# Two heads at a time on the row halves of TensorE: the sparse scores of a two-layer streaming encoder

## The reference

```python
def _dsa_attend(q, k, v, iq, ik, iw, cid_q, cid_k, k_top):
    sc = jnp.einsum('bqhd,bkd->bqhk', iq, ik).astype(jnp.float32)
    score = jnp.einsum('bqhk,bqh->bqk', jax.nn.relu(sc), iw.astype(jnp.float32)) * IDX_SCALE
    ...
    _, sel = lax.top_k(score, kk)
    ...
    s = jnp.einsum('bqhd,bqsd->bqhs', q, k_sel).astype(jnp.float32) * (HD_C ** -0.5)
    s = jnp.where(valid[:, :, None, :], s, -jnp.inf)
    p = jax.nn.softmax(s, axis=-1).astype(v.dtype)
    return jnp.einsum('bqhs,bqsd->bqhd', p, v_sel)
```

## Time and profile before

| | us |
|---|---|
| median of 3 runs (lowest to highest) | 2138.87 (2136.68 to 2142.58) |
| the profiled execution | 2146.08 |
| its span | 2144.4 |
| TensorE busy | 1932.9 |
| VectorE busy | 1392.8 |
| ScalarE busy | 736.3 |
| mean granted TensorE clock | 0.982 |

### The profile page before, as it was taken

How to read it: one execution, slowest core, us unless ns; L and a number is a source line. 1 busy time by engine, 2 the same in 40 slices (tenths; PEclk the granted TensorE clock), 3 DMA queues, 4 the chain that set the end, 5 groups by cost and what they waited for, 6 DMA issues and landing times. The chain is left out here.

```text
span 2144.4 us, 27310 instructions
## 1 busy us (share of the span) xinstructions
PE 1932.9 (90%) x9670; PEld 1083.1 (51%) x9690; DVE 1392.8 (65%) x2961; ACT 736.3 (34%) x1678; POOL 259.0 (12%) x360
## 2 busy tenths in 40 slices
PE   3999999989999788999959999999899988889997
PEld 2634457555545555654444344565554455565443
DVE  3268488998796776533233684989897956665322
ACT  3353134233212544443243512334331134444332
POOL 0000132342100000001100002233221000000011
PEclk9999999999999999999979999999999999999998
DMA  8201214121323003223351022221205130022242
GB/s 281 99 25 67 79 47 136 61 81 50 113 73 77 18 6 94 89 67 132 128 193 55 25 71 74 92 97 60 96 30 153 38 72 13 26 76 87 95 149 103
DMA packets 151272, 178.34 MB, mean 83 GB/s; under 512 B 71408, under 2 KB 106736, under 8 KB 150864
## 3 DMA queue, kind: packets, MB, share of 16 engines
q1 hardware_dynamic: 123072, 139.19, 20.7%
q10 hardware_dynamic: 28064, 37.38, 4.9%
HBM read 119.72 MB, written 66.69 MB: 87 GB/s over the span
## 5 line engine op out<-in xcount | busy, mean ns | idle before, releaser
L914 PE MATMUL ps<-wring,xnT_arena 128*128 128x512 f32 (+2 forms) x2304 | 921.3, 542 | 0.0
L914 PEld LDWEIGHTS ps<-wring,xnT_arena 128*128 128x128 f32 x2304 | 405.0, 192 | 354.5 <-issue 337.7
L1759 DVE TENSOR_SCALAR_CACHE_REDUCE arena<-arena,theta 32x1056 bf16<-32x1056 f32 x496 | 461.3, 979 | 2.3
L1396 ACT COPY arena<-ps 128x512 f32<-128x512 f32 (+3 forms) x144 | 75.3, 523 | 449.4 <-PE ps L914 415.8
L1274 PE MATMUL ps<-wring,xnT_arena 128*128 128x512 f32 x512 | 223.9, 595 | 0.0
L2043 DVE TENSOR_REDUCE mneg<-ps 128x1 f32<-128x192 f32 (+9 forms) x148 | 113.9, 770 | 87.1 <-PE ps L1206 84.7
L1274 PEld LDWEIGHTS ps<-wring,xnT_arena 128*128 128x128 f32 x512 | 96.4, 191 | 115.4 <-issue 115.4
L1050 PEld LDWEIGHTS ps<-arena 128*128 128x128 f32 x488 | 69.6, 193 | 106.8 <-DVE arena L1866 78.2
L2206 POOL TENSOR_TENSOR arena<-arena 128x1024 f32<-128x1024 f32 (+1 forms) x16 | 35.5, 2216 | 727.2 <-DVE arena L1984 539.1
L1050 PE MATMUL ps<-arena 128*128 128x128 f32 x488 | 80.2, 287 | 39.5 <-DVE arena L1866 39.3
L1361 ACT COPY xnT_arena<-ps 128x512 f32<-128x512 f32 (+3 forms) x84 | 39.0, 464 | 188.9 <-PE ps L1218 141.6
(11 more groups left out here) (270 smaller groups left out, 2495.1 us busy)
## 6 DMA issues: line engine op xcount, KB each, us to landing
projected<-arena ACTq DMA_DIRECT2D x130, 256.0 KB, 2.0
arena<-residual SPq DMA_DIRECT2D x34, 512.0 KB, 5.2
wring<-in_w_in SPq DMA_DIRECT2D x16, 1024.0 KB, 7.6
o_bc<-projected SPq DMA_DIRECT2D x36, 384.0 KB, 3.7
wring<-in_w_in SPq DMA_DIRECT2D x6, 2048.0 KB, 8.8
wring<-in_w_out SPq DMA_DIRECT2D x8, 1024.0 KB, 5.5
residual<-arena SPq DMA_DIRECT2D x16, 512.0 KB, 2.6
out<-arena SPq DMA_DIRECT2D x16, 512.0 KB, 4.0
```

The lines of the kernel that those rows point to most:

```text
L914: o = mm(bank(pbank(k), 0, w_), xnT[:, c, t * P:(t + 1) * P], w, start=(c == 0), stop=(c == CH - 1))
L1396: nc.scalar.copy(stage[s][:, 0:wide], bank(pbank(k), 0, wide)).then_inc(p_ev, 1)
L1759: V.tensor_scalar(cmp_out[0][r, (i % 2) * WMAX:(i % 2) * WMAX + uw[u]], score[u][r], th_, 0.0, op, ALU.add, accum_out=into[r, i:i + 1]).th ...
```

## The change

For the paired tiles of dsa, heads 0 and 1 (then 2 and 3) become one unit of the order. The keys stand twice, on rows 0 to 63 and again on rows 64 to 127. Two heads of queries stand on the same halves, so the queries of a tile need two transposes in place of four. For each run of keys two matmuls of 64 rows follow each other, one head on the upper and one on the lower half of the rows, into different banks. Then the masks of the first head follow, on all 128 rows, and those of the second. The score of tile 8, which has no partner, stays one head at a time but now uses rows 0 to 63 alone, since the other half no longer holds zeros. Fox and unit "s" keep their form.

```diff
+        packed = lambda mu: mu[0] == "dsa" and any(len(group) == 2 and mu[1] in group for group in UNIT_GROUPS)
...
+                elif packed((m, group[0])):
+                    AJ += [(m, u, 2 * g + e) for g in range(2) for u in group for e in range(2)]
...
+            if packed(j[:2]) and j[2] % 2 == 0:
+                score_at.append(max([n - 3] + score_at[-1:] + [i + (0 if i >= n - 1 or packed(AJ[i][:2]) else 1) for k in (n, n + 1) for i in used_before[AJ[k]]]))
...
-                for m, u, h in AJ[max(0, n - 1):n]:
-                    if u == "s" or h % 2:
+                now = [j for i, j in enumerate(AJ) if (j[1] == "s" or j[2] % 2) and n == i + 1 + (packed(j[:2]) and i + 2 < len(AJ) and packed(AJ[i + 2][:2]))]
+                for m, u, h in now:
...
+                                    if u == "p":
+                                        tr(ps[0:HD, 512 * b + P * i:512 * b + P * i + P], src, C("ident"))
+                                        o = mm(ps[HD:P, 512 * b + P * i:512 * b + P * i + P], src, C("ident"), start=True, stop=True, skip_group_check=True)
...
+                            if packed(mu):
+                                for g in range(2):
+                                    o = tr(bank(b, P * g, P), QD_[unit_no[mu] % 2][:, P * g:P * g + P], C("ident"))
...
+                        if packed(mu):
+                            for key, w, col in runs:
+                                for e, h_ in enumerate(heads):
+                                    at = col - base + 512 * banks_of((m, u, h_))[0]
+                                    mm(ps[:, at:at + w], qt[HD * e:HD * e + HD, h // 2, :], dsaKT["p"][HD * e:HD * e + HD, key:key + w],
+                                       start=True, stop=False, skip_group_check=True)
+                        for h_ in heads if packed(mu) else ():
...
+                        if m == "dsa" and u != "s":
+                            qt, kt = qt[0:HD], kt[0:HD]
...
-                        copy(dsaKT["p"][0:HD, 0:HALF], ps[0:HD, 512 * b:512 * b + HALF]).then_inc(own_sem, one_more(own))
+                        copy(dsaKT["p"][:, 0:HALF], ps[:, 512 * b:512 * b + HALF]).then_inc(own_sem, one_more(own))
...
-                    nc.gpsimd.memset(dsaKT["p"][HALF:], 0.0).then_inc(pool_own, one_more(own))
```

More of the change, by code:

```diff
@@ L375, in encoder @@
         AU = [(m, u) for m in ("fox", "dsa") for group in UNIT_GROUPS for u in group]
-        AJ = [(m, u, h) for m in ("fox", "dsa") for group in UNIT_GROUPS for h in (range(H) if group != ["s"] else [0]) for u in group]
+        packed = lambda mu: mu[0] == "dsa" and any(len(group) == 2 and mu[1] in group for group in UNIT_GROUPS)
+        AJ = []
+        for m in ("fox", "dsa"):
+            for group in UNIT_GROUPS:
+                if group == ["s"]:
+                    AJ.append((m, "s", 0))
+                elif packed((m, group[0])):
+                    AJ += [(m, u, 2 * g + e) for g in range(2) for u in group for e in range(2)]
+                else:
+                    AJ += [(m, u, h) for h in range(H) for u in group]
         group_of = {(m, u): (m, i) for m in ("fox", "dsa") for i, group in enumerate(UNIT_GROUPS) for u in group}
@@ L505, in plan_attend @@
             for n, job in enumerate(AJ):
-                seq += [("score", AJ[i]) for i in range(n + 1, len(AJ)) if score_at[i] == n == i - 1]
+                seq += [("score", AJ[i]) for i in range(n + 1, len(AJ)) if score_at[i] == n == i - 1 and not packed(AJ[i][:2])]
                 seq.append(("turn", job))
                 seq += [("exp", AJ[i]) for i in (n + 1, n + 2) if i < len(AJ) and i == (max(n, 0) + 2 if score_at[i] <= i - 3 else n + 1)
-                        and ("exp", AJ[i]) not in seq]
+                        and ("exp", AJ[i]) not in seq and ("score", AJ[i]) in seq]
                 done, backs = backs, []
@@ L526, in plan_attend @@
                 seq += [("back", p) for p in done]
-                seq += [("score", AJ[i]) for i in range(n + 1, len(AJ)) if score_at[i] == n < i - 1]
+                seq += [("score", AJ[i]) for i in range(n + 1, len(AJ)) if score_at[i] == n and (n < i - 1 or packed(AJ[i][:2]))]
+                seq += [("exp", AJ[i]) for i in range(n + 1, len(AJ)) if score_at[i] == n == i - 1 and packed(AJ[i][:2])]
             PV.append((AJ[-1][0], AJ[-1][1], AJ[-1][2] // 2))
@@ L1145, in scores @@
                         mu, n = (m, u), job_no[(m, u, h)]
+                        if packed(mu) and h % 2:
+                            return
+                        heads = (h, h + 1) if packed(mu) else (h,)
                         base = 512 * banks_of((m, u, h))[0]
@@ L1160, in scores @@
                                     evacuated(a)
-                        for i in sorted(used_before[m, u, h]):
+                        for i in sorted(set(i for e in heads for i in used_before[m, u, e])):
                             turned(AJ[i])
```

38 lines of the change are left out of this document (30 added, 8 removed).

## The result

The changed kernel takes 2153.47 us (median of 6 runs, 2150.0 to 2158.11) against 2138.28 before: ratio 1.0071, 95% interval 1.0054 to 1.0087. It is slower by 15 us; 2128 was forecast, at most 2140. The profiled execution of the changed kernel took 2154.23 us (span 2152.6, clock 0.974); that of before, 2146.08, lies 8 above its median, so the two profiles differ by only 8.

What follows compares the result with a forecast made beforehand. TensorE was taken as the bound, with VectorE's queue limiting (1, 5) and (2, 6). Per layer +2.0 - 2.2 + 0.5 - 4.3 - 4.3 + 3.0 = -5.3, both -10.6: 2138.9 to 2128 us, range 2112 to 2140.

Steps and rivals of the forecast that it cites:

- rival C: Slower: more, shorter TensorE waits drop the clock to 1.2 GHz more often, 1.7 us per stretch; 2152 to 2155; chance 9%.
- (1, 5): dsa's pair of tiles 1 and 5: VectorE's queue limits it, so +0.5 us per layer where TensorE's work alone gives -3.0.
- beside the path: Preparations: wider key copies, ScalarE's query scaling, query DMA and the dropped memset add no time; at worst a few tenths.
- (2, 6): dsa's pair of tiles 2 and 6: rounds set by VectorE, long wait cut into several; -4.3 us per layer.
- (3, 7): dsa's pair of tiles 3 and 7: bound by TensorE, keeps its gain; -4.7 + 0.4 for changes = -4.3 us per layer.
- The scores: Paired dsa tiles 0 to 7: two heads abreast halve 27.3 us of score time, -13.65 us per layer.
- Changes of division: Switching TensorE's array between row divisions costs 0.09 us each: +1.5 per layer at paired masks, +2.2 in tile 8.
- tile 8: dsa's unpaired tile: 24 changes of array division and a first score waiting for VectorE's copy; +3.0 us per layer.
- Keys: Second key product for nine dsa tiles, made in fox and partly hidden by a wait: +2.0 us per layer, bounds 0 to 3.7.
- cover: In tiles 3 and 7, the small tile's values, over 1 us, hide the wait for the copy of turned probabilities.
- (0, 4): dsa's pair of tiles 0 and 4: TensorE's work gives -2.1 + 0.4 - 0.4; taken as -2.2 us per layer.
- rival B: Emptying PSUM, one bank set per tile, takes back nearly all gain but that of tiles 3 and 7; 2139; chance 20%.

Runs made afterwards that it cites:

- e2: Changed kernel's order of jobs (two heads as one unit) without halves: all scores on 128 rows, one after the other, keys once; 2149.9 us, ratio 1.0033 to 1.0063.
- e10: Kernel before with only the dsa keys written to both halves of the rows, scores still on 128 rows in the old order; 2144.2 us, ratio 1.0001 to 1.0032.
- e1: Changed kernel with tile 8 scored on all 128 rows again, ScalarE zeroing the upper rows of its queries; 2142.8 us, ratio 1.0006 to 1.0034.
- e3: Kernel before with the scores of all dsa prompt tiles on rows 0 to 63, one head at a time, old order; 2196.4 us, ratio 1.0196 to 1.0292.
- e17: Kernel before with the dsa scores of tiles 3 and 7 alone on rows 0 to 63, old order; 2144.0 us, ratio 1.0015 to 1.0038.
- e16: Kernel before with the dsa scores of tiles 1 and 5 alone on rows 0 to 63, old order; 2147.0 us, ratio 1.0011 to 1.0063.
- e19: Changed kernel, joined order throughout, but tiles 0, 4, 1, 5 and 8 scored on 128 rows, GpSimd zeroing; 2145.6 us, ratio 1.0012 to 1.0047.
- e7: Changed kernel with tiles 0 and 4 in the old order on 128 rows, tile 8 on 128 rows, ScalarE zeroing query rows; 2150.5 us, ratio 1.0036 to 1.0075.
- e11: Changed kernel with tiles 0 and 4 in the old order on 128 rows, tile 8 on 128 rows, GpSimd zeroing query rows; 2142.9 us, ratio 1.0012 to 1.0037.
- e14: As e11, with the next pair's query transposes moved behind the score of their step; 2145.7 us, ratio 1.0016 to 1.0051.
- e18: Changed kernel, joined order throughout, but tiles 0, 4 and 8 scored on 128 rows, GpSimd zeroing; 2142.6 us, ratio 1.0003 to 1.0025.
- e15: Kernel before with the dsa scores of tiles 0 and 4 alone on rows 0 to 63, old order; 2148.4 us, ratio 1.0026 to 1.0065.

## Why the prediction was wrong

The step that failed is the clock: the sum had no term for more time at 1.2 GHz, and held rival C at 9% because (1, 5) had 1.00 with 2.2 us of waits. The runs show 54 us more at 1.2 GHz, worth 21 us (at 0.39) to 27 (at 0.5). A second step failed with it, that the preparations are "beside the path": in (1, 5), (2, 6) and (3, 7) TensorE now waits 0.9 to 1.3 us for ScalarE's copy of the next queries, which it did not before.

By the table of medians, with 0.5 us for each at 1.2 GHz: the order +7.9 (e2), the keys +4.6 (e10), tile 8 +1.7 (after less e1), and 54 us more at 1.2 GHz, +27.1. What is left to reach the measured +14.4 (against before's 2139.1) is -26.9 for the pairs abreast; that is a remainder (e1 less before, e2 and e10), so that the sum closes proves nothing. With 0.39, the clock is 21 and the rest -7. At equal clock the change gains 7 to 13 us; -10.6 was forecast. That the extra time at 1.2 GHz comes with the half rows is shown: 62 us with the keys alone (e10), 69 with the order alone (e2), 103 with the pairs abreast on top (e1), 156 with half rows and no new order (e3), against 64 before.

- *The scores* (half of 27.3 per layer, 27.3 in all): close to the remainder of 26.9, which holds the query transposes and the changes of division too; no run took these apart. In (3, 7) a joined score of 960 columns takes 2.04 us to its masks, 0.42 more than one head's 1.62, where the forecast put 0.09 for one change.
- *Changes of division* at 0.09: measured 0.12 (e17). For tile 8 I had +3.0; its 29.3 us less half of 6.8 is 25.9, +1.8. The other 3.4 of its +5.2 are clock, which the step did not have.
- *Keys* +2.0: 2.3 per layer. Right.
- *(1, 5)* +0.5: -0.6 and -0.8. *(2, 6)* -4.3: -3.8. Close. The drawing by hand of VectorE's queue was right in kind: 15.48 of 19.00 and 19.44 of 22.17 us busy, neither over the nine tenths I had asked for.
- *(3, 7)* -4.3: -2.1. That the small tile's values "cover" VectorE's copy of the turned probabilities held here: both large paired scores start without a wait (L1230 at 897.91 above). In (1, 5) and (2, 6) such copies do hold a paired score up, by 2.08 and 1.55 us. What (3, 7) lost is in two parts. TensorE's work shrank by 3.8 (25.11 to 21.31 us busy), and its idle time grew from 0.7 to 2.4. e2 pays 2.1 here without any half rows. The largest wait is the turning back of the values behind the copy of tile 8's queries, which the forecast had "beside the path"; the other is tile 8's first score, which waited 0.52 before:
```profile
885.97 0.30 PE L1312 MATMUL ps<-cf,xnT_arena 128*128 128x128 f32 x1 [1.32 <-ACT arena L1639]
...
905.61 0.40 PE L1254 MATMUL ps<-arena 64*128 64x64 f32 x2 [0.72 <-ACT xnT_arena L1411]
```
- *(0, 4)* -2.2: with the entry +3.8 and +2.7. The step "TensorE's work gives -2.1 + 0.4 - 0.4" took the first score to start where it did; e2 shows +4.6 for the entry by the order alone, at a clock of 1.00. My first window began at the pair's first score, so a score that comes 5 us later in the order could not show in it.
- *C*: 2152 to 2155 was its price and 2153.5 came, which is luck in part: it priced seven or eight new stretches of 3.4 us per layer, by new waits. From the sample to the output's end the two profiles show 7 such stretches before and 9 after; but they last 17 and 20 us in (0, 4) and 6.8 around tile 8. And what I held against C, (1, 5) with 2.2 us of waits at 1.00, was work on all rows.

The Trainium skill (TensorE: Matmul & The Clock Gate, section What's actually happening) has the gate follow how busy TensorE has been: sustained work brings 2.4 GHz back. By that, e3's (1, 5) should be at 2.4 GHz; the trace has 35.72 of 36.66 us busy at 0.50, and the measurement decides. The rule of the Trainium skill on emptying PSUM (TensorEngine Tiling, section PSUM Bottleneck), which I had weighed for rival B, is seen in the waits for copies, but it did not decide: (2, 6), which B gave -2, lost 3.8, and the joined order with all its waits costs 8 us (e2).

What stays open: (1, 5), entered at 2.4 GHz, has no time at 1.2 GHz with half rows alone (e16) nor with the joined order alone (e2, e19), and 7 to 10 us with both where the pair is the first abreast (e7, e11, e14), 3.4 in e18. That fits a wait that starts a stretch and half rows that keep it, but which wait starts it there was not tried. Nor was it tried why (0, 4) of e15 has 6.8 us in layer 2 where layer 1 has 20.5, and each of these stage figures is from one profile.

## What to carry to other kernels

Two half-row products abreast take half of TensorE's time only if the clock holds: read the granted clock at each wait next to the place, and ask what would follow if the stretch at 1.2 GHz there lasted five times as long. Joining two steps into one unit also joins their conditions; price the entry, from the last instruction of the stage ahead, and the places where a resource changes hands (here the bank of the turned queries), before the steady rounds. And compare kernels by their clocks over many runs: one profile here was 8 us off its median, half of the effect.

## What the runs showed of the hardware

- A stage with half-row fp32 products ran at 1.2 GHz for 68.3 us in one stretch, TensorE busy 66.9 of them (e3, layer 1); the same kind of work entered at 2.4 GHz in (3, 7) stayed there (e17, 28.65 us at 1.00).
- Two fp32 products of two records each on the two row halves ran abreast: 2.04 us to the masks for two heads of 960 columns, against 1.62 for one on all rows.
- A change between 64 and 128 rows cost 0.12 us (e17: 2.85 us for 24).
- The kernel's run-to-run spread is mostly clock: 0.39 us for each us at 1.2 GHz, correlation 0.85 over 117 runs.
